# Latent attention with the outputs of two heads side by side on 64 array columns each, and probabilities divided on GpSimd before they are transposed

## The reference

```python
def mla_attend(qn, qr, kn, kr, v):
    scale = (MLA_NOPE + MLA_ROPE) ** -0.5
    s = jnp.einsum('bhqd,bhkd->bhqk', qn, kn) + jnp.einsum('bhqr,bkr->bhqk', qr, kr)
    p = jax.nn.softmax(s.astype(jnp.float32) * scale, axis=-1)
    return jnp.einsum('bhqk,bhkv->bhqv', p.astype(v.dtype), v)
```

## Time and profile before

| | |
|---|---|
| device time, median of 3 runs | 2204.05 us (2202.57 to 2205.18) |
| span of the profiled execution (first to last instruction) | 2201.9 us |
| median of the runs less the span | 2.15 us |
| TensorE busy | 2140.6 us, 97% |
| VectorE busy | 1397.2 us, 63% |
| ScalarE busy | 870.3 us, 40% |
| GpSimd busy | 67.8 us, 3% |
| mean granted TensorE clock | 0.994 |

### The profile page before, as it was taken

One profiled execution on the slowest core, in us unless ns is written; L12 is line 12 of the kernel. 1 busy time (PEld: TensorE's weight loads), 2 busy tenths in 40 slices (PEclk: granted clock), 3 DMA queues, 4 the chain that ended last, 5 costly groups with the idle time before them and its releaser, 6 DMA issues.

```text
span 2201.9 us, 30377 instructions
## 1 busy us (share of the span) xinstructions
PE 2140.6 (97%) x12124; PEld 1863.2 (85%) x12124; DVE 1397.2 (63%) x2396; ACT 870.3 (40%) x1503; POOL 67.8 (3%) x78
## 2 busy tenths in 40 slices
PE   6999999999999999999999999999999999999998
PEld 3888888987888888888888898888888888999998
DVE  5789986675563334566877656676647655468554
ACT  4321223545463223442222352222236544546444
POOL 0000001000000000100000000000010000000001
PEclk9999999999999999999999999999999999999999
DMA  7545554321212222334454324355523223254553
GB/s 278 202 167 175 210 184 135 138 75 34 61 66 95 88 99 73 124 134 144 163 182 155 122 97 142 132 204 202 178 99 124 76 89 118 96 192 172 178 197 124
DMA packets 76747, 304.07 MB, mean 138 GB/s; under 512 B 7488, under 2 KB 15424, under 8 KB 60224
## 3 DMA queue, kind: packets, MB, share of 16 engines
q1 hardware_dynamic: 57600, 234.79, 30.7%
q10 hardware_dynamic: 19008, 67.35, 8.5%
HBM read 297.92 MB, written 4.19 MB: 137 GB/s over the span
## 4 chain that ended last, share of the span: by engine, by line
PE 68%; DVE 4%; ACT 3%; issue 1%; DMA 0%; DVEq 0%; ACTq 0%
PE ps L604 20%; PE ps L606 20%; PE ps L605 20%; DVE w_lo L1841 1%; PE ps L1064 1%; ACT w_hi L1212 1%; PE ps L934 1%; PE ps L1118 1%; PE ps L920 0%; PE ps L1108 0%; PE ps L942 0%; PE ps L923 0%; PE ps L922 0%; PE ps L1052 0%; PE ps L664 0%
## 5 line engine op out<-in xcount | busy, mean ns | idle before, releaser
L1212 ACT CAST w_hi<-w_raw 128x1024 fp32r<-128x1024 f32 (+5 forms) x516 | 443.8, 871 | 982.6 <-PE ps L606 644.6
L604 PE MATMUL ps<-xn_hi,w_hi 128*128 128x512 f32 (+1 forms) x2272 | 802.0, 353 | 22.1 <-DVE xn_lo L1996 7.6
L1841 DVE TENSOR_TENSOR w_lo<-w_raw,w_hi 128x1024 fp32r<-128x1024 f32 (+5 forms) x516 | 515.2, 1004 | 470.5 <-ACT w_hi L1212 468.1
L606 PE MATMUL ps<-xn_lo,w_hi 128*128 128x512 f32 (+1 forms) x2272 | 792.0, 349 | 0.0
L605 PE MATMUL ps<-xn_hi,w_lo 128*128 128x512 f32 (+1 forms) x2272 | 791.9, 349 | 0.0
L604 PEld LDWEIGHTS ps<-xn_hi,w_hi 128*128 128x128 f32 x2272 | 431.8, 190 | 81.9 <-issue 18.0
L606 PEld LDWEIGHTS ps<-xn_lo,w_hi 128*128 128x128 f32 x2272 | 431.4, 190 | 55.2
L605 PEld LDWEIGHTS ps<-xn_hi,w_lo 128*128 128x128 f32 x2272 | 432.0, 190 | 52.6
L604 PE MATMUL ps<-split_scratch,w_hi 128*128 128x512 f32 (+2 forms) x1100 | 380.9, 346 | 3.4 <-DVE split_scratch L2058 1.0
L606 PE MATMUL ps<-split_scratch,w_hi 128*128 128x512 f32 (+2 forms) x1100 | 378.0, 344 | 0.0
L605 PE MATMUL ps<-split_scratch,w_lo 128*128 128x512 f32 (+2 forms) x1100 | 377.9, 344 | 0.0
(11 more groups left out here) (192 smaller groups left out, 1594.0 us busy)
## 6 DMA issues: line engine op xcount, KB each, us to landing
w_raw<-in_up SPq DMA_DIRECT2D x86, 1024.0 KB, 4.8
ada_w<-in_ada ACTq DMA_DIRECT2D x128, 512.0 KB, 4.5
w_raw<-in_dn SPq DMA_DIRECT2D x32, 768.0 KB, 4.7
w_raw<-in_merge SPq DMA_DIRECT2D x32, 768.0 KB, 4.3
w_raw<-in_dn SPq DMA_DIRECT2D x32, 640.0 KB, 4.2
w_raw<-in_proj SPq DMA_DIRECT2D x20, 1024.0 KB, 4.7
w_raw<-in_wout SPq DMA_DIRECT2D x16, 512.0 KB, 3.6
w_raw<-in_gate SPq DMA_DIRECT2D x8, 1024.0 KB, 4.7
```

The lines of the kernel that those rows point to most:

```text
L604: nc.tensor.matmul(out, w_hi, hi, start=first, stop=False)
L606: return nc.tensor.matmul(out, w_hi, lo, start=False, stop=last)
L1212: nc.scalar.copy(wh[:, u % 2, h, 0:w], raw[:, u % RAW, h, raw_first(u + i * per):raw_first(u + i * per) + w]).then_inc(hi_ready, 1)
L1841: nc.vector.tensor_tensor(wl[:, u % 2, h, 0:w], raw[:, u % RAW, h, raw_first(u + i * per):raw_first(u + i * per) + w], wh[:, u % 2, h, 0:w ...
```

## The change

1. The probabilities are divided before they are transposed. VectorE's reciprocal now releases GpSimd, which multiplies the item's probabilities in place (48 new instructions, 512 or 256 columns wide), and TensorE's transposes wait for GpSimd instead of for the exponentials.
2. ScalarE copies the transposed probabilities of both items of a head side by side (`turned_probs`).
3. The outputs are computed for a pair of heads and 256 queries at once, values as weights (64 columns) and probabilities streamed (256 columns): head 2p on array columns 0 to 63, head 2p+1 on columns 64 to 127. The result has features on partitions. They stand at the step at which the last item of the pair's second head was due: four latent and four context groups in layer 0, four latent groups in layer 1.
4. VectorE takes a group out of PSUM with one copy of 128x256 (12 in place of 48 multiplications of 128x64). The 24 transposes back and their banks are gone; the high and low parts are made from SBUF.
5. The Fourier step waits, as before, for all outputs; the last of them now comes directly ahead of it.

```diff
+            def head_pairs(l):
+                groups, per = [], len(item_list(l, 1)[0])
+                for p in range(MLA_HEADS // 2):
+                    for c, (cols, nk) in enumerate([(LAT, TOK)] + ([(CTX, CTX_LEN)] if l < DEPTH - 1 else [])):
+                        groups.append((p, cols, nk, (2 * p + 1) * per + 2 * c + 1))
+                return groups
@@ TensorE
-                def token_outputs(t):
-                    h, _, _, _, nk = items[t]
+                def pair_outputs(g):
+                    p, _, nk, t = groups[g]
                     pe.wait_ge(wt_ready, a0 + t + 1)
                     banks = B_OT[l]
-                    if t >= len(banks):
-                        pe.wait_ge(o_ready, done["pair"] + t + 1 - len(banks))
+                    if g >= len(banks):
+                        pe.wait_ge(o_ready, done["pair"] + g + 1 - len(banks))
                     for kc in range(nk // P):
-                        ins = nc.tensor.matmul(ps[:, banks[t % len(banks)], 0:MLA_VD], WT4[:, t % 4, kc, :],
-                                               Vt[:, kc, h * MLA_VD:(h + 1) * MLA_VD], ...)
+                        for j in range(2):
+                            h, rows = 2 * p + j, slice(MLA_VD * j, MLA_VD * j + MLA_VD)
+                            out = ps[rows, banks[g % len(banks)], 0:2 * P].rearrange("p (t n) -> p t n", t=2)
+                            ins = nc.tensor.matmul(out, Vt[:, kc, h * MLA_VD:(h + 1) * MLA_VD], turned_probs(l, h, nk)[:, :, kc, :],
+                                                   start=(kc == 0), stop=(kc == nk // P - 1), tile_position=(0, MLA_VD * j))
...
-                        pe.wait_ge(exp_done, a0 + t - 1)
+                        pe.wait_ge(probs_ready, n0 + t - 1)
                         transposes(a0 + t - 2, items[t - 2][4], Pm[:, (t - 2) % 3])
-                    if t >= 3:
-                        token_outputs(t - 3)
+                    if pair_ended_by(l, t - 3) is not None:
+                        pair_outputs(pair_ended_by(l, t - 3))
...
-                for c in range(4):
-                    pe.wait_ge(o_ready, done["pair"] - (3 - c) * 2 * len(item_list(l, 1)[0]))
-                    for tk in range(cols.start, cols.stop, P):
-                        ins = nc.tensor.transpose(ps[:, B_Y[c], tk:tk + P], YT[:, tk // P, c * P:(c + 1) * P], ident[:])
-                    ins.then_inc(turned_back, 1)
@@ ScalarE
-                        nc.scalar.copy(WT4[:, (t - 2) % 4, 0:nk // P, :],
+                        nc.scalar.copy(turned_probs(l, h, nk)[:, tq],
                                        ps[:, B_TR, 0:nk].rearrange("p (k n) -> p k n", n=P)).then_inc(wt_ready, 1)
...
-                    act.wait_ge(turned_back, 4 * l + c + 1)
-                    nc.scalar.copy(YMh[:, c, cols], ps[:, B_Y[c], cols]).then_inc(ymhi_ready, 1)
+                    act.wait_ge(o_ready, done["pair"] - (3 - c) * len(streams(both)))
+                    nc.scalar.copy(YMh[:, c, cols], Y[:, c, cols]).then_inc(ymhi_ready, 1)
@@ GpSimd
+                for t, (_, _, _, _, nk) in enumerate(items):
+                    pool.wait_ge(inverse_ready, n0 + t + 1)
+                    nc.gpsimd.tensor_scalar(Pm[:, t % 3, 0:nk], Pm[:, t % 3, 0:nk], rr[:, (a0 + t) % 8, 0:1], None, ALU.mult
+                                            ).then_inc(probs_ready, 1)
@@ VectorE
-                        nc.vector.reciprocal(rr[:, b, 0:1], sm[:, b, 0:1]).then_inc(dve_chain, 1)
+                        nc.vector.reciprocal(rr[:, b, 0:1], sm[:, b, 0:1]).then_inc(inverse_ready, 1)
-                    if t >= 4:
-                        dve.wait_ge(pv_done, done["pair"] + t - 3)
-                        nc.vector.tensor_scalar(YT[:, col // P, h * MLA_VD:(h + 1) * MLA_VD],
-                                                ps[:, B_OT[l][(t - 4) % len(B_OT[l])], 0:MLA_VD],
-                                                rr[:, (a0 + t - 4) % 8, 0:1], None, ALU.mult).then_inc(o_ready, 1)
+                    g = pair_ended_by(l, t - 4)
+                    if g is not None:
+                        dve.wait_ge(pv_done, done["pair"] + g + 1)
+                        nc.vector.tensor_copy(Y[:, p, cols], ps[:, B_OT[l][g % len(B_OT[l])], 0:2 * P]).then_inc(o_ready, 1)
...
-                    nc.vector.tensor_tensor(YMl[:, c, cols], ps[:, B_Y[c], cols], YMh[:, c, cols].bitcast(F32),
+                    nc.vector.tensor_tensor(YMl[:, c, cols], Y[:, c, cols], YMh[:, c, cols].bitcast(F32),
                                             ALU.subtract).then_inc(ymlo_ready, 1)
```

More of the change, by code:

```diff
@@ L457, in item_list, with pair_ended_by, probs_before, turned_probs @@
             return items, pairs
+        def head_pairs(l):
[4 more added lines that the diff above has]
+            return groups
+        def pair_ended_by(l, t):
+            for g, (_, _, _, item) in enumerate(head_pairs(l)):
+                if item == t:
+                    return g
+            return None
+        def probs_before(l):
+            return sum(len(item_list(k, MLA_HEADS)[0]) for k in range(l))
+        def turned_probs(l, h, nk):
+            if l == DEPTH - 1:
+                home = (SC[:, 0:1024], SC[:, 1024:2048], SD[:, 0:1024])[h % 3]
+            elif nk == TOK:
+                home = SC[:, 1024 * (h % 2):1024 * (h % 2) + 1024]
+            else:
+                home = SD[:, 512 * (h % 2):512 * (h % 2) + 512]
+            return home.rearrange("p (t k n) -> p t k n", t=2, k=nk // P)
+        def home_used(l, h, nk):
+            if l == DEPTH - 1:
+                return (h - 3) // 2 + 1 if h >= 3 else 0
+            return 2 * (h // 2 - 1) + (nk != TOK) + 1 if h >= 2 else 0
         def head_at(l, t):
@@ L1036, in mla_attention @@
             def mla_attention(l):
-                items, pairs = item_list(l, MLA_HEADS)
-                a0, g0 = done["item"], done["pair"]
+                items, groups = item_list(l, MLA_HEADS)[0], head_pairs(l)
+                a0, n0 = done["item"], probs_before(l)
                 mla_head(l, 1)
@@ L1632, in mla_attention @@
             def mla_attention(l):
-                items, pairs = item_list(l, MLA_HEADS)
-                a0, g0 = done["item"], done["pair"]
+                items = item_list(l, MLA_HEADS)[0]
+                a0 = done["item"]
                 for t in range(-1, len(items) + 2):
@@ L1758, in _ @@
         def _(pool):
-            done = dict(norm=0, chunk=0, chain=0)
+            done = dict(norm=0, chunk=0, chain=0, item=0)
             def link(ins):
@@ L2434, in mla_attention @@
             def mla_attention(l):
-                items, pairs = item_list(l, MLA_HEADS)
-                a0, g0 = done["item"], done["pair"]
-                inverted = []
+                items, groups = item_list(l, MLA_HEADS)[0], head_pairs(l)
+                a0 = done["item"]
                 for t in range(-1, len(items) + 4):
@@ L2465, in mla_attention @@
                 done["item"] += len(items)
-                done["pair"] += len(items)
+                done["pair"] += len(groups)
             link(nc.vector.memset(cz[:], 0.0))
```

30 lines of the change are left out of this document (14 added, 16 removed).

## The result

The changed kernel takes 2207.11 us (median of 20 runs, 2204.11 to 2212.22), the kernel before 2202.8 (20 runs, 2198.45 to 2205.18): a ratio of 1.0025, 95% interval 1.0018 to 1.0032. It is slower by 4.3 us in the medians and by 5.5 by the ratio; I had forecast 1.4 us faster, and no measurable change. (The 2202.6 us of the forecast are counted from the 2204.05 of three runs; against the 2202.8 of twenty they would be 2201.4.) The changed kernel's runs fall into two groups, 13 from 2204.1 to 2207.9 and seven from 2211.5 to 2212.2; its profiled execution is one of the first group.

What follows compares the result with a forecast made beforehand. The prediction held that ScalarE and VectorE pace the heads although TensorE is 97% busy. Layer 0 -0.1 and layer 1 -1.3 made -1.4 us, from the median 2204.05 to 2202.6 us, range 2194 to 2209.

Steps and rivals of the forecast that it cites:

- a rival at 0.12: Layer 1 steps 4, 8, 12 and layer 0's end: idle TensorE lowers its clock, 1.5 us each, four 2208.6; chance 0.12.
- The prediction's own sign of being wrong: Wrong if two heads of layer 1 take under 12.5 us, or the granted clock shows more low stretches than before.
- Output matmuls: Both layers' attention: records run two at a time; latent pair 1.97 us, context pair 1.11, with mode changes.
- Chain-bound in layer 1: Layer 1: ScalarE and VectorE chain sets 12.98 us per two heads; removing outputs gives 0, TensorE waits for gate copy.
- End of layer 1: Layer 1's last steps to the Fourier step: ends at 1904.9 against 1906.21, -1.3 us, bounds -2.5 and 0.
- Heads with a latent pair: Layer 0, every second head: latent outputs stand before the last scores, 6.25 us to projection, +0.3 each, twice.
- Heads with a context pair: Layer 0, the other heads: VectorE's copy delays the key split, chain 0.4 late, projection at 5.75, -0.3 each, twice.
- GpSimd's price: Division between reciprocal and transposes: 1.0 us for 512 columns, 0.6 for 256, bounds 0.5 and 1.3.
- End of layer 0: Layer 0 from step 26 to the Fourier step: 13.9 us against 13.43, taken as +0.4.
- VectorE beside GpSimd: Layer 0: VectorE's splits may stand still beside GpSimd's division; taken 0, up to +1 if it reaches step 26.
- TensorE's own ledger: TensorE's work: 27 us of outputs become 20.2, 2.6 of transposes go; about 14 us saved were TensorE the bound.
- the rival that has TensorE as the bound: Whole kernel: all TensorE time freed comes off, 14 us, 2190; chance 0.20 together with half of it.

Runs made afterwards that it cites:

- warm_l1: Changed kernel plus 16 extra identity transposes behind the score transposes of layer 1's steps 4, 8 and 12: 2204.1 us, ratio 1.0006.
- the division alone: Kernel before with only the division moved: GpSimd multiplies the probabilities ahead of their transposes, outputs as they were: 2206.6 us, ratio 1.0011.
- the diagonal: Changed kernel, layer 1 waits filled, probabilities transposed by matmul with a diagonal of reciprocals made by VectorE (2217.5 us) or GpSimd (2215.9 us).
- the thin outputs: Kernel before with only the first of four key chunks in each of layer 1's 16 output groups: 2202.1 us, ratio 0.9997.
- no_division: Changed kernel with the division left out, transposes waiting for the exponential alone: 2205.3 us, ratio 1.0012.
- vector_divides: Changed kernel with VectorE instead of GpSimd doing all 48 multiplications, behind the reciprocal: 2210.7 us, ratio 1.0035.

## Why the prediction was wrong

The step that failed is the sum: its terms, -0.1 for layer 0 and -1.3 for layer 1, hold nothing for TensorE's clock, which was left to a rival at 0.12. I had worked it out there: waits of 2.2 us at steps 4 and 8, a longer one at step 12, a thinner end of layer 0, 1.5 us for each fall, 2208.6 for four. The waits came as described, 2.09, 2.09 and 3.55 us. So did the falls: three in layer 1 and one at the end of layer 0. But the one at step 12 is not new, so three new falls cost 1.5, 1.5 and 2.7 us, where the rival had four at 1.5; that it came near the measured 2207.1 is in part two errors that cancel. The prediction's own sign of being wrong showed as well: between 550 and 1900 us the trace has five low stretches of the clock, that of the kernel before three.

My ground for the low chance was "the projections between are dense". The earlier trace rows spoke against that discount: around 1876.80 the projections were as dense, TensorE waited 1.9 us, and the clock fell. Filling the waits of the attention and nothing else moved the time from 2207.1 to 2200.3, under the kernel before, so the clock is shown as the cause of the loss; that the falls of 1.5 us are in the chain is shown by warm_l1. What is not split is how much of the loss in the medians comes from falls behind the new waits, and how much from falls behind waits that every version has (at 922 us and at layer 1's first scores).

The Trainium skill, page TensorE: Matmul & The Clock Gate, section Part 1: The HAM clock gate, says that the number of slow matmuls at a kernel's start differs between runs of one kernel. The runs here show the like in mid-kernel (878.5 or 882.4 us for the same code), and that is why single traces mislead on this question.

The other terms of the prediction:

- *Output matmuls*: right. Sixteen records take 1.95 us, the next plain matmul comes 1.88 after their start (forecast 1.97); behind a context pair 1.01 (1.11).
- *Chain-bound in layer 1*: right. The 12.98 us that the prediction calls two heads' steps are one head's two steps (7 and 8 in the earlier trace rows). With the change they take 12.86 where no fall lies between (1840.94 to 1853.80), and TensorE waits for the gate copy.
- *End of layer 1*: forecast -1.3, from the scores behind step 12 to the Fourier step. It is -1.7, 22.14 us before and 20.42 with the change, both at full clock:

```profile
1884.07:1906.21 22.14, 20.77 (x178) 1.00 0.31 103
```

```profile
1886.91:1907.33 20.42, 19.12 (x154) 1.00 0.30 104
```

- *Layer 0, first head*: -0.7 (forecast -0.5). *Heads with a latent pair*: +0.25 each (+0.3). *Heads with a context pair*: +0.03, not -0.3. I followed their chain through VectorE's key split. It goes through ScalarE, as the timeline of the changed kernel shows:

```profile
614.16 1.08 PE L1102 MATMUL ps<-scratch 128*64 128x256 f32 x8
...
616.61 0.59 ACT L1680 COPY scratch<-ps 128x512 f32<-128x512 f32 x1 [0.82 <-PE ps L969]
...
617.09 0.60 ACT L1660 ACTIVATE split_scratch<-ps 96x512 fp32r<-96x512 f32 x1
...
617.58 0.68 ACT L1521 ACTIVATE x_res<-ps,score_negmax 128x512 f32<-128x512 f32 x1
...
618.41 0.39 PE L1087 MATMUL ps<-split_scratch 96*128 96x256 f32 x1 [0.66 <-ACT x_res L1521]
```

The second copy waits for transposes that stand behind the pair, and the rounding of the queries and the exponential queue behind that copy.

- *GpSimd's price*: 1.57 and 0.93 us, above my bound of 1.3. I had placed one input between a fill and a two-input addition, which was no argument: one input with a scalar took longer than two inputs (1.29). The Trainium skill's rule (GPSIMD Engine Reference, Engine selection), one-input work at about line rate, does not hold here either, with VectorE at 0.49 us for the same tile. The mis-sized term cost little: heads of layer 0 are as long with GpSimd dividing as without division, and the end of layer 0 got 0.55 to 0.6 us.
- *End of layer 0*: forecast +0.4 from step 26. From the last projection on it is 24.17 + 0.4 (pairs, with the clock up) + 0.55 (division) + 2.66 (clock) = 27.78. A fall is dearer here than my 1.5: outputs, transposes and their waits all stand in the chain.
- *VectorE beside GpSimd*: expected 0, and it was. Two multiplications that ran beside a split took 2.13 and 2.17 us (at 619.17 and 599.74), both under a projection.
- *TensorE's own ledger*: the "27 us of outputs" are a slip. 320 records at the 0.82 us for eight that the prediction uses make 32.8. The forecast does not rest on it, but the rival that has TensorE as the bound should have stood 6 us lower than 2190.

What stays open: why a given wait makes the clock fall in one execution and not in the next; what parts the changed kernel's runs into groups near 2206 and 2212; why the clock fell more often with the division alone; and how much of the diagonal's 12 us is the longer transposes and how much the two buffers.

## What to carry to other kernels

Before taking work off TensorE in a stage that another engine's chain bounds, list the waits that will be left, and look in the trace of before for a wait of that length and what the granted clock did behind it. Shorter waits close together count too: the thin outputs left 1.15 and 0.33 us. One such case outweighs a general argument. Where the freed time has no use, cheap transposes into an idle bank, placed exactly in the wait, held the clock up here; two microseconds beside it they only cost their own time. And since falls come and go between executions, compare each run's mean clock as well as one trace with another.

## What the runs showed of the hardware

Waits of about 2 us (2.08, 2.09, 2.54) were followed by the lower clock in some executions and not in others: the one at 922 us in 7 of the 15 traces where it was unfilled, the one at layer 1's first scores in 8 of 12. With the change and without filling, layer 1 had three falls in each of three traces: behind steps 4, 8 and 12 in the changed kernel's, behind the first scores and steps 8 and 12 in the two others (no_division, vector_divides). Behind steps 4 and 8 the clock fell at none of the 20 places that were filled. Behind step 12 it fell in four of the five traces where filling left a wait of 1.80 us, and in none of the five where it left 1.36 us or less. Behind the wait at 922 the low stretch was 10.2 us long in four traces and cost 3.8 to 4.0 us; in three it was 3.4 us long and cost 0.3 to 0.5.

A wait is not the only thing ahead of a fall. In all 18 traces the clock also fell between 554 and 560 us. TensorE does not stand still there; it runs, or has just run, 32 matmuls of two columns each (here in the changed kernel, the fall at 558.0):

```profile
554.14 3.63 PE L690 MATMUL ps<-mean_weights,scratch 128*128 128x2 f32 x32
```

GpSimd's multiplication by a per-partition scalar takes 1.57 us for 128x512 fp32 and 0.93 for 128x256; VectorE's 0.49 and 0.35. An fp32 matmul with a diagonal costs two records where the transpose costs one.
